# Row scales spread from a repeated column, and an attention entered without the layer norm ahead of it, in a fused four-layer fp32 kernel

## The reference, cut to what matters

```python
def first_block(...):                      # two layers
    for l in range(DEPTH):
        hn = rms_norm(h, norm_mix_pre[l])
        ...                                # dilated attention, short conv, gated delta net
        h = h + rms_norm(mix, norm_mix_post[l])
        ...                                # memory cross-attention
        h = h + rms_norm(xa, norm_xattn_post[l])
        ...                                # swiglu FFN
        h = h + rms_norm(swiglu_ffn(...), norm_ffn_post[l])

def conformer_conv(val, glu_gate, silu_gate, dw_w, dw_b, ln_g, ln_b):
    u = val * jax.nn.sigmoid(glu_gate)
    u = depthwise_conv_31(u, dw_w) + dw_b
    u = jax.nn.silu(layer_norm(u, ln_g, ln_b))
    return u * jax.nn.silu(silu_gate)

def odd_mixer(h_lat, h_ctx, ...):          # second block, second layer
    cv, cgl, cg, dq, dk, dv, dg = split_cols(h_lat @ w_in, ODD_WIDTHS)
    ...                                    # the same of the context
    oc = conformer_conv(cv, cgl, cg, dw_w, dw_b, ln_g, ln_b)
    ...                                    # od: neighbourhood attention of 8 heads with a bias table
    return concatenate([oc, od * silu(dg)]) @ w_out
```

## Time and profile before

| | |
|---|---|
| median of 3 runs | 2654.5 us |
| the profiled execution | 2654.48 us, its span 2652.5 us |
| mean granted clock of PE | 0.989 |
| PE busy | 2549.2 us, 96% |
| DVE busy | 1672.7 us, 63% |
| ACT busy | 1137.1 us, 43% |

### The profile page before, as it was taken

The page is one execution under the profiler, slowest core; times in us unless marked ns, Lnnn a source line. Parts: engine busy times, 40 slices in busy tenths (PEclk is TensorE's granted clock), DMA queues, the critical chain, the costliest instruction groups (busy, mean ns, idle before and its releaser), DMA issues.

```text
span 2652.5 us, 34668 instructions
## 1 busy us (share of the span) xinstructions
PE 2549.2 (96%) x13244; PEld 2032.9 (77%) x13244; DVE 1672.7 (63%) x3243; ACT 1137.1 (43%) x2084; POOL 0.2 (0%) x4
## 2 busy tenths in 40 slices
PE   8999999999999999999999999999999999999898
PEld 6878888678888778688877788887866667787566
DVE  7666665464447785665743644487486666599664
ACT  4336443442332343463544423323346666323553
POOL 0000000000000000000000000000000000000000
PEclk9999999999999999999999999999999999999999
DMA  4220033123227422201421223464110001122311
GB/s 164 84 72 17 23 129 119 37 75 103 96 96 237 152 88 84 64 1 48 151 72 56 80 96 96 148 220 142 56 41 17 17 17 35 62 72 72 66 54 48
DMA packets 74083, 219.37 MB, mean 83 GB/s; under 512 B 21312, under 2 KB 21568, under 8 KB 73152
## 3 DMA queue, kind: packets, MB, share of 16 engines
q1 hardware_dynamic: 48384, 176.29, 20.4%
q10 hardware_dynamic: 25536, 40.87, 5.0%
HBM read 215.03 MB, written 2.10 MB: 82 GB/s over the span
## 4 chain that ended last, share of the span: by engine, by line
PE 82%; DVE 11%; ACT 3%; issue 2%; ACTq 1%; DMA 0%; DVEq 0%
PE bank L579 20%; PE bank L581 19%; PE bank L580 19%; PE bank L846 4%; PE bank L810 4%; DVE c_y L2319 3%; PE bank L820 3%; DVE w_lo L545 2%; PE bank L1424 1%; PE bank L1411 1%; PE bank L610 1%; PE bank L612 1%; PE bank L611 1%; DVE e_s L909 1%; ACT w_hi L538 1%
## 5 line engine op out<-in xcount | busy, mean ns | idle before, releaser
L579 PE MATMUL bank<-a_hi,w_hi 128*128 128x512 f32 (+1 forms) x1480 | 591.1, 399 | 20.8 <-DVE w_lo L545 14.8
L538 ACT ACTIVATE w_hi<-w_raw 128x1024 fp32r<-128x1024 f32 x334 | 352.9, 1060 | 570.0 <-PE bank L581 535.4
L581 PE MATMUL bank<-a_hi,w_lo 128*128 128x512 f32 (+1 forms) x1480 | 578.4, 391 | 0.0
L580 PE MATMUL bank<-a_lo,w_hi 128*128 128x512 f32 (+1 forms) x1480 | 577.9, 390 | 0.0
L545 DVE TENSOR_TENSOR w_lo<-w_raw,w_hi 128x1024 fp32r<-128x1024 f32 x334 | 407.7, 1223 | 250.3 <-ACT w_hi L538 249.5
L579 PEld LDWEIGHTS bank<-a_hi,w_hi 128*128 128x128 f32 (+1 forms) x1480 | 277.4, 187 | 92.4 <-issue 17.2
L581 PEld LDWEIGHTS bank<-a_hi,w_lo 128*128 128x128 f32 (+1 forms) x1480 | 277.3, 187 | 60.9
L580 PEld LDWEIGHTS bank<-a_lo,w_hi 128*128 128x128 f32 (+1 forms) x1480 | 277.7, 188 | 60.1 <-issue 3.4
L579 PE MATMUL bank<-b_hi,w_hi 128*128 128x512 f32 x704 | 258.9, 368 | 1.0 <-DVE w_lo L545 0.8
L580 PE MATMUL bank<-b_lo,w_hi 128*128 128x512 f32 x704 | 250.3, 356 | 0.0
L581 PE MATMUL bank<-b_hi,w_lo 128*128 128x512 f32 x704 | 249.0, 354 | 0.0
(11 more groups left out here) (416 smaller groups left out, 3985.1 us busy)
## 6 DMA issues: line engine op xcount, KB each, us to landing
w_raw<-w_tiles SPq DMA_DIRECT2D x334, 512.0 KB, 3.5
mod_raw<-mod_tiles ACTq DMA_DIRECT2D x48, 512.0 KB, 4.3
d_bias<-rpb_rows ACTq DMA_DIRECT2D x16, 224.0 KB, 4.8
hT<-xT ACTq DMA_DIRECT2D x8, 256.0 KB, 6.3
m_in<-memT ACTq DMA_DIRECT2D x2, 1024.0 KB, 4.7
mod_cond<-cond_rows ACTq DMA_DIRECT2D x2, 1024.0 KB, 6.3
out<-hT ACTq DMA_DIRECT2D x8, 256.0 KB, 2.2
ctx_sq<-ctxT ACTq DMA_DIRECT2D x1, 1024.0 KB, 7.5
```

The costliest lines, as they stand in the source:

```text
L538: act.activation(w_hi[:, t % SPLIT, :], w_raw[:, t % RAW, :], ACT.Copy).then_inc(sem("w_rounded"), 1)
L579: pe.matmul(o, wh, hi[:, k, :n], start=k == 0, stop=False)
L580: pe.matmul(o, wh, lo[:, k, :n], start=False, stop=False)
L581: mm = pe.matmul(o, wl, hi[:, k, :n], start=False, stop=k == kc - 1)
```

## The change

1. No diagonals any more. PE takes the column itself, repeated 128 times with stride zero, as stationary operand and the identity (for the decays the triangular matrix "upto") as moving one, four matmuls of 128 columns into a bank. The operations of L696, L705, L711, L1634, L1679, L1809 and L1900 and the waits for them are gone; reciprocals stay.
2. The transposes of v and ACT's copies of them move into the projection, behind dq0. The bias fetches of heads 0 and 1 and of the mask are issued behind cl1, those of heads 2 and 3 at unit 5 of the attention, and the first bias addition stands at the end of DVE's projection work.
3. The attention starts at once. The convolution's layer norm is spread over its units: sums at step 4, the mean on ACT at unit 8, centring on DVE at units 9 to 12, squares on ACT at 11, 12, 15 and 16, sums of squares at steps 7 and 10 (their bank is held from one to the other), the root at 19, the reciprocal in four pieces at 20 to 23, scaling at 24 to 27, the silus among those of the gates in the tail. The eight dummies are gone.

```diff
-        def spread_dve(dve, key, n):
+        def inverse_dve(dve, key, n):
             m = n // P
             dve.wait_ge(*when("rms", *key))
             dve.reciprocal(col[:, 4:4 + m], col[:, 0:m]).then_inc(*done("rrms", *key))
-            dve.wait_ge(*when("rrms", *key))
-            for t in range(m):
-                op = dve.tensor_scalar(spread[:, P * t:P * t + P], ident, col[:, 4 + t:5 + t], None, ALU.mult)
-            op.then_inc(*done("spread", *key))
...
+        def column_rows_pe(pe, out, columns, diagonal):
+            for t, column in enumerate(columns):
+                mm = pe.matmul(head(out, t), column.broadcast_to([P, P]), diagonal, start=True, stop=True)
+            return mm
...
         def rstd_pe(pe, key, n, hold=False):
-            pe.wait_ge(*when("spread", *key))
+            pe.wait_ge(*when("rrms", *key))
             b = claim(pe, "rstd", *key, hold=hold)
-            pe.matmul(b[:, :n], ones, spread[:, :n], start=True, stop=True).then_inc(*filled("rstd", *key))
+            column_rows_pe(pe, b, [col[:, 4 + t:5 + t] for t in range(n // P)], ident).then_inc(*filled("rstd", *key))
...
         def gdn_rows_pe(pe, l, n, parts=(0, 1)):
             for w in parts:
-                pe.wait_ge(*when("diag_decay" if w == 0 else "diag_beta", l, n))
+                pe.wait_ge(*when("g" if w == 0 else "beta_rk2", l))
                 b = claim(pe, "row", l, n, w)
-                pe.matmul(b[:, :], ones, diag_of(w, n), start=True, stop=True).then_inc(*filled("row", l, n, w))
+                column_rows_pe(pe, b, [colnh(GL if w == 0 else BR, n, h) for h in range(GH)],
+                               C("upto") if w == 0 else ident).then_inc(*filled("row", l, n, w))
...
+        ln_row = rstd[:, :]
+        MEAN_STEP, VAR_STEPS = 4, (7, 10)
+        MEAN_UNIT, SQUARE_UNITS, STD_UNIT = 8, (11, 12, 15, 16), 19
...
+        def conformer_between_dve(dve, u, taps):
+            next(taps, None)
+            next(taps, None)
+            if u == MEAN_UNIT - 1:
+                for _ in taps:
+                    pass
+            c = u - MEAN_UNIT - 1
+            if 0 <= c < CC:
+                dve.wait_ge(*when("c_mean"))
+                dve.tensor_tensor(c_y[:, c, :], c_y[:, c, :], ln_row, ALU.subtract).then_inc(*done("c_centred", c))
+            q = u - STD_UNIT - 1
+            if 0 <= q < TT:
+                dve.wait_ge(*when("c_std"))
+                dve.reciprocal(ln_row[:, P * q:P * q + P], ln_row[:, P * q:P * q + P]).then_inc(*done("c_rstd", q))
+            c = u - STD_UNIT - 1 - TT
+            if 0 <= c < CC:
+                dve.wait_ge(*when("c_rstd", TT - 1))
+                dve.scalar_tensor_tensor(out=c_y[:, c, :], in0=c_y[:, c, :], scalar=G("ln_g", c), in1=ln_row,
+                                         op0=ALU.mult, op1=ALU.mult).then_inc(*done("c_scaled", c))
...
         def odd_tail_act(act, u):
+            if u == 5:
+                for h in (2, 3):
+                    load_bias(act, h)
             if u == ODD_LAST:
                 for c in range(CC):
+                    conformer_silu_act(act, c)
                     odd_silu_act(act, c)
...
             odd_in_pe(pe)
-            conformer_pe(pe)
-            odd_turn_pe(pe)
-            warm_pe(pe, 8, "odd_att")
             attention_pe(pe, ("odd",), odd_units(), d_s, pair_tiles(d_pt),
                          lambda kt, h: [d_vt[:, kt, AD * h:AD * h + AD]],
                          need=[("d_vt_in", 5), ("dq", CC - 1), ("dk", CC - 1, "ctx")],
-                         fill=odd_gate_steps(pe), blocks=lambda i: 4)
+                         fill=odd_gate_steps(pe), blocks=lambda i: 4,
+                         at={MEAN_STEP: lambda: conformer_mean_pe(pe),
+                             VAR_STEPS[0]: lambda: conformer_var_pe(pe, 0),
+                             VAR_STEPS[1]: lambda: conformer_var_pe(pe, 2)})
```

More of the change, by code:

```diff
@@ L1506, in out_row_pe @@
         def out_row_pe(pe, l, n):
-            pe.wait_ge(*when("o_diag", l, n))
+            pe.wait_ge(*when("o_inv", l, n))
             b = claim(pe, "o_row", l, n)
-            pe.matmul(b[:, :], ones, (spread if n % 2 == 0 else sqacc)[:, :], start=True, stop=True)\
-              .then_inc(*filled("o_row", l, n))
+            column_rows_pe(pe, b, [colnh(L2, n, h) for h in range(GH)], ident).then_inc(*filled("o_row", l, n))
         def square_act(act, l, name):
@@ L1625, in gdn_act @@
                 split_act(act, o_t[:, h, :], 4 + h, ("out", l))
[L1627 to L1631, removed]
-                act.wait_ge(*when("bank_filled", "row", l, n - 2, 1))
-            for h in range(GH):
-                op = act.activation(head(diag_of(1, n), h), ident, ACT.Copy, scale=colnh(BR, n, h))
-            op.then_inc(*done("diag_beta", l, n))
         def out_rms_act(act, l, n):
@@ L2339, in conformer_dve, with conformer_mean_pe @@
                         next(taps, None)
[L2340 to L2357 removed]
+                if name == "dq1":
+                    bias_dve(dve, 0)
+            return taps
+        def conformer_mean_pe(pe):
             b = claim(pe, "c_sum")
@@ L2362, in conformer_pe, with conformer_var_pe @@
             mm.then_inc(*filled("c_sum"))
-            b = claim(pe, "c_var")
-            for c in range(CC):
-                pe.wait_ge(*when("c_sq", c))
-                mm = pe.matmul(b[:, :], ones, sq[:, c % 2, :], start=c == 0, stop=c == CC - 1)
-                mm.then_inc(*(filled("c_var") if c == CC - 1 else done("c_sq_used", c)))
-        def conformer_act(act):
-            for c in range(CC):
-                act.wait_ge(*when("c_centred", c))
-                if c >= 2:
-                    act.wait_ge(*when("c_sq_used", c - 2))
-                act.activation(sq[:, c % 2, :], c_y[:, c, :], ACT.Square).then_inc(*done("c_sq", c))
-            b = bank(act, "c_var")
-            act.activation(spread[:, :], b[:, :], ACT.Sqrt, bias=C("eps"), scale=1.0 / (CC * P))\
-               .then_inc(*freed("c_var", also=("c_std",)))
-            for c in range(CC):
-                act.wait_ge(*when("c_scaled", c))
-                act.activation(c_y[:, c, :], c_y[:, c, :], ACT.Silu, bias=G("ln_b", c)).then_inc(*done("c_silu", c))
+        def conformer_var_pe(pe, first):
+            b = claim(pe, "c_var", hold=True) if first == 0 else banks[book.known.jobs["c_var",][0] if book.known else 0]
+            for c in (first, first + 1):
+                pe.wait_ge(*when("c_sq", c))
+                mm = pe.matmul(b[:, :], ones, ln_sq(c), start=c == 0, stop=c == CC - 1)
+                mm.then_inc(*(filled("c_var") if c == CC - 1 else done("c_sq_used", c)))
+            if first:
+                book.release("c_var")
@@ new lines, in conformer_mean_act, with conformer_square_act, conformer_std_act @@
+        def conformer_mean_act(act):
+            b = bank(act, "c_sum")
+            act.activation(ln_row, b[:, :], ACT.Copy, scale=1.0 / (CC * P)).then_inc(*freed("c_sum", also=("c_mean",)))
+        def conformer_square_act(act, c):
+            act.wait_ge(*when("c_centred", c))
+            if c >= 2:
+                act.wait_ge(*when("c_sq_used", c - 2))
+            act.activation(ln_sq(c), c_y[:, c, :], ACT.Square).then_inc(*done("c_sq", c))
+        def conformer_std_act(act):
+            b = bank(act, "c_var")
+            act.activation(ln_row, b[:, :], ACT.Sqrt, bias=C("eps"), scale=1.0 / (CC * P))\
+               .then_inc(*freed("c_var", also=("c_std",)))
@@ new lines, in conformer_silu_act, with conformer_between_act @@
+        def conformer_silu_act(act, c):
+            act.wait_ge(*when("c_scaled", c))
+            act.activation(c_y[:, c, :], c_y[:, c, :], ACT.Silu, bias=G("ln_b", c)).then_inc(*done("c_silu", c))
+        def conformer_between_act(act, u):
+            if u == MEAN_UNIT:
+                conformer_mean_act(act)
+            for c in range(CC):
+                if u == SQUARE_UNITS[c]:
+                    conformer_square_act(act, c)
+            if u == STD_UNIT:
+                conformer_std_act(act)
```

139 lines of the change are left out of this document (44 added, 95 removed).

## The result

| | before | after |
|---|---|---|
| median | 2655.4 us (4 runs, 2654.2 to 2658.0) | 2628.7 us (4 runs, 2625.8 to 2631.7) |
| ratio, 95% interval | | 0.9898 (0.9881 to 0.9915) |
| the profiled execution, span | 2652.5 us | 2625.0 us |
| mean granted clock there | 0.989 | 0.992 |

What follows compares the result with a forecast made beforehand. PE was taken as the bound, busy 2549.2 of 2652.5 us. Row scales from a column (-3.1) and direct entry into the odd attention (-12.2) summed to -15.3 us, so 2639 us from 2654.5; range 2631 to 2650.

Steps and rivals of the forecast that it cites:

- Price on PE: At 43 row-scale sites, four 128-column matmuls replace one of 512: +0.03 us each at 34 PE-bound sites, +1.0 us.
- R3: Rival at the 43 row-scale sites: repeated column loads slower or unhidden, up to 0.68 us each, 2667 us; chance 0.07.
- The five uncovered norms: Post-norms of cross-attention and FFN in both layers, and final norm: row matmul starts earlier without diagonals, 5 x 0.5 = -2.5 us.
- Elsewhere at nothing: Remaining diagonals, at pre-norms and the 16 decay and beta rows: hidden beside other work, so removal gains nothing.
- Part A: Row scales from a column instead of diagonals at 43 sites: -3.1 us; also measured alone, odd layer as before.
- The entry: Start of the odd layer's attention: DVE's first maximum at 2443.7 instead of 2468.96, -25.3 us.
- The sign of 146 to 148 us: Expected time from end of the odd projection to first output product, instead of 159 us, if the forecast is right.
- Unit 5: In the odd attention: ACT's four more bias fetches delay its later work and PE waits, +2.2 us (ends 0 and 4.4).
- The sums and bank 7: Odd attention: layer norm's channel sums on PE, +7.0 us; step 10's scores wait for ACT's root to free the bank, +2.5.
- The tail: End of the odd attention: the convolution's four silus stand between the gate's, half of 2.71 us hidden, +1.4 us.
- R1: Rival: layer norm inside the attention not covered; two more stops with slow clock cost about 9, 2648 us; chance 0.22.
- R2: Rival: stops at unit 5 and step 10 hide, clock fall after the entry goes away, 2632 us; chance 0.14.

## Why the prediction was wrong

Forecast: -15.3 us in the sum, of which nothing for clock. Measured: -26.7.

- **Price on PE, right.** Eight records follow at 0.11 us and a repeated column loads in 190 ns. R3 (2667) fell. The spacing rule of the Trainium skill (TensorE: Matmul & The Clock Gate, Back-to-back issue gap), cited there with an estimate of 2693, doesn't hold for these fp32 rows.
- **The five uncovered norms, right** as waiting: putting the stop back costs 2.0 us at full clock, where 2.5 were taken. It missed that at one of them the stop of 0.34 us also went with low clock behind it.
- **"Elsewhere at nothing", wrong in one place.** With two diagonals on DVE ahead of the second layer's first attention PE's stop there is 1.65 us, without them 1.11.
- **Part A** was -3.1 and is -2.5 at full clock (2621.7 to 2619.2), but 12.7 us in the medians. The difference is mostly clock (the rest falls from 30.6 to 21.7).
- **The entry, right as waiting; another 2.7 us there are clock.** I moved the first maximum by 25.3 us and PE's step 2 with it. In the traces the first maximum is where it was forecast: 4.3 us behind the projection, 4.5 forecast. But PE's step 2 starts 5.4 us behind it (2437.64 to 2443.01), where it was 7.1 (2468.96 to 2476.04): PE doesn't stop for step 1, and its clock stays up. Of the 7.1, 2.7 were matmuls at the lower level: the first scores behind the stop took 1.22 us instead of 0.70, and the twelve matmuls behind them 5.2 (2470.86 to 2476.04) instead of 2.95 (2440.06 to 2443.01). The sign of 146 to 148 us for the stretch didn't follow from the sum: with the 2.8 us of transposes moved out of it, the sum gives 144. Measured are 135.1.
- **Unit 5, wrong.** 2.2 us were taken from the one stop of the earlier trace rows; nothing is there. That row was a bad price. Its 4.37 us held one fetch of 2.28; ordinary fours of the attention take 2.8 to 3.1 us (3.3 once) and stop PE for 0.6 to 0.8 at the later place and not at all at unit 5.
- **The same stop in the kernel before, not seen as a cost that could go.** 2.17 us of waiting and a clock of 0.89 in its window. In the changed kernel 0.76 is left at full clock. Step 11 to the next turn took 10.1 us (2540.78 to 2550.87) and takes 5.8 (2516.65 to 2522.47): 1.4 us less of waiting and 2.9 less of low clock.
- **The sums and bank 7, right**: +7.0 taken, 3.5 for the mean's and two of 1.8 for the variance's measured; +2.5 taken, 2.28 measured. The activation behind the table load starts 0.01 us after it (2505.98 + 1.28, then 2507.27), so the 1.4 us more that the prediction estimated from a drain are not seen.
- **The tail, right in size by luck**: +1.4 taken, 1.3 measured (from the last step's turn to the output product 15.7 us before, 17.0 after). But 1.2 of the 1.3 are matmuls at the lower level, 5.39 and 3.15 us where 4.50 and 2.84 stand before; PE's two waits are the same within 0.1 us. In the other six kernels with these silus in the tail the second wait is 1.95 to 2.79 us, and 1.27 or 1.28 in every kernel without them, so there they seem to cost up to 1.5 us.

**The step that failed** is the sum's silence on the clock: a term put at nothing without a reason. I read 0.91 and 0.89 in two windows behind stops, priced such a fall at 3 us, and used it only in R1 and, once, in R2. Measured, the clock's part is 7.0 us (30.6 to 23.6); without it the changed kernel would stand at some 2636, inside the range. The second term that failed is unit 5, 2.2 us booked and none there; with the 1.4 us of the stop near 2544 it would cover the 3.1 us by which the gain at full clock exceeds the sum; the scatter of the runs doesn't let this be shown. R2 had the right direction (2632) and was too small: its fall behind the entry and its stop at unit 5 went as it said, its stop at step 10 stayed.

Four places of the kernel before lost their fall in the changed one's profile: near 550, near 1087, behind the entry, near 2544 us. So did two near 1407 and 1465 us, the second behind one of the five norms; and the changed kernel has falls near 50, 180, 497 and 2214 us that this profile of the kernel before lacks (its second profile has three of these four). So the sum of 7.0 us is measured, and its division among the places is not shown.

## What to carry to other kernels

Price a stop that is removed as its waiting and the low clock behind it, both read from the trace, since in a PE-bound kernel the second can exceed the first: at the stop of 2.17 us here 1.4 us of waiting went and 2.9 us of low clock. Take a wait's price from several rows of its kind: an outlier in one profile can belong to the program, not to chance, and be undone by an edit elsewhere. Test the parts of a two-part change alone; here the larger part's main gain came from an early fetch and early transposes, and the elaborate half, the spread layer norm, gave some 2.5 us until the bank it held was released later.

## What the runs showed of the hardware

- At one place a stop of 0.34 us of PE, with a longer one of 1.4 to 2.1 us behind it, went with a fall of its granted clock (0.89 against 1.00 over 15 us) in five of five profiles; without the short stop the clock fell in one of eight. At two other norms it was five of five against three and five of eight. Filling longer stops left the time the same. What sets the falls over the whole kernel stays open.
- A stationary operand that is one column with stride zero loads in the same 190 ns as a tile.
- A DMA issue on ACT took 1.46, 2.28 and 2.40 us where its neighbours take 0.7, each time with an instruction load of another queue starting within it; one fetch with such a load took 0.60, and the next 1.28. Why is open.
- The kernel before varies from 2649.0 to 2661.4 us over all its runs, more than its first three runs (2654.2 to 2656.3) suggested. Differences under 3 us between the medians of kernels of 4 to 5 runs, like 2623.6 and 2624.6, mean little by themselves; that holds for the 2.5 us of the spread norm too.
